# A named ScalarE table for logarithm and exponential in gated linear attention, and one pair of evictions moved

## The reference, cut to what matters

```python
la_f = jax.nn.log_sigmoid(lr_f @ w_g_f + b_g_f) / GLA_TAU      # gate, both directions
b = jnp.cumsum(gc, axis=-2)                                    # per chunk of 64 tokens
q_in = qc * jnp.exp(b - ref);  k_in = kc * jnp.exp(ref - b)
q_inter = qc * jnp.exp(b);     k_state = kc * jnp.exp(b_last - b)
decay = jnp.exp(b_last[..., 0, :])
...
o = rmsnorm(o_f + o_b, out_norm)                               # y / sqrt(mean(y*y) + eps)
y_gla = gla_branch(...) * jax.nn.silu(gate_g)
y_mla = mla_branch(...) * jax.nn.silu(gate_a)
```

## Time and profile before

| what | value |
|---|---|
| median of 3 runs | 2426.88 us (2423.91 to 2427.3) |
| profiled execution, its own time | 2427.41 us |
| its span, first to last instruction | 2425.6 us |
| PE busy | 2254.9 us, 93% of the span |
| DVE busy | 1390.4 us, 57% |
| ACT busy | 1132.1 us, 47% |
| POOL busy | 488.1 us, 20% |
| mean granted TensorE clock | 0.975 |

### The profile page before, as it was taken

One profiled execution on the slowest core, in us unless ns is written; L12 is line 12 of the kernel. 1 busy time (PEld: TensorE's weight loads), 2 busy tenths in 40 slices (PEclk: granted clock), 3 DMA queues, 4 the chain that ended last, 5 costly groups with the idle time before them and its releaser, 6 DMA issues.

```text
span 2425.6 us, 30125 instructions
## 1 busy us (share of the span) xinstructions
PE 2254.9 (93%) x11196; PEld 1781.9 (73%) x11196; DVE 1390.4 (57%) x2137; ACT 1132.1 (47%) x1768; POOL 488.1 (20%) x512
## 2 busy tenths in 40 slices
PE   8998888988999993999999999999899999999998
PEld 4777555864777762777877888888777877888886
DVE  4578378325777766367426776354457526776353
ACT  5222377223666654566453445245656453445142
POOL 1046434111223222311230002001211230002000
PEclk9999999999999995999999999999999999999999
DMA  6200120124999976111110003112111110003112
GB/s 204 100 35 1 57 83 1 11 104 163 381 395 381 340 295 227 40 31 35 36 46 22 12 28 133 49 53 100 41 36 35 35 46 22 12 10 133 67 52 96
DMA packets 148397, 239.56 MB, mean 99 GB/s; under 512 B 45232, under 2 KB 101808, under 8 KB 136368
## 3 DMA queue, kind: packets, MB, share of 16 engines
q1 hardware_dynamic: 138304, 221.07, 25.9%
q0 software_dynamic: 8928, 16.80, 1.8%
q10 hardware_dynamic: 1040, 0.00, 0.0%
HBM read 212.13 MB, written 41.42 MB: 105 GB/s over the span
## 4 chain that ended last, share of the span: by engine, by line
PE 52%; ACT 4%; DVE 3%; issue 2%; POOL 1%; DMA 0%; POOLq 0%; ACTq 0%; DVEq 0%
PE ps L105 11%; PE ps L106 11%; PE ps L107 11%; PE ps L95 4%; PE ps L1998 2%; PE ps L1952 1%; PE ps L1951 1%; PE ps L1950 1%; PE ps L1989 1%; PE ps L1988 1%; PE ps L1986 1%; PE ps L1985 1%; PE ps L1987 1%; PE ps L524 1%; PE ps L1866 1%
## 5 line engine op out<-in xcount | busy, mean ns | idle before, releaser
L107 PE MATMUL ps<-HT_hi,WF_lo 128*128 128x512 f32 x800 | 314.6, 393 | 0.0
L105 PE MATMUL ps<-HT_hi,WU_hi 128*128 128x512 f32 x704 | 285.3, 405 | 18.7 <-POOL WF_lo L1028 6.4
L106 PE MATMUL ps<-H_lo,WU_hi 128*128 128x512 f32 x704 | 276.5, 393 | 0.0
L106 PE MATMUL ps<-WT_lo,HT_hi 128*128 128x512 f32 x664 | 260.5, 392 | 0.0
L1028 POOL TENSOR_TENSOR WF_lo<-WF,WU_hi 128x1024 fp32r<-128x1024 f32 x42 | 110.8, 2638 | 466.2 <-ACT WU_hi L1299 466.2
L105 PE MATMUL ps<-W_hi,HT_hi 128*128 128x512 f32 x472 | 186.9, 396 | 2.9 <-DVE WT_lo L2568 2.9
L107 PE MATMUL ps<-W_hi,MIX_lo 128*128 128x512 f32 x480 | 188.4, 393 | 0.0
L107 PEld LDWEIGHTS ps<-HT_hi,WF_lo 128*128 128x128 f32 x800 | 151.8, 190 | 32.6
L105 PEld LDWEIGHTS ps<-HT_hi,WU_hi 128*128 128x128 f32 x704 | 133.9, 190 | 52.6 <-POOL WF_lo L1028 8.6
L106 PEld LDWEIGHTS ps<-H_lo,WU_hi 128*128 128x128 f32 x704 | 134.0, 190 | 29.5 <-issue 2.9
L106 PEld LDWEIGHTS ps<-WT_lo,HT_hi 128*128 128x128 f32 x664 | 125.8, 190 | 25.6 <-issue 0.5
(11 more groups left out here) (482 smaller groups left out, 5682.7 us busy)
## 6 DMA issues: line engine op xcount, KB each, us to landing
WT<-in_w_gate SPq DMA_DIRECT2D x31, 1024.0 KB
WT<-in_w_up SPq DMA_DIRECT2D x31, 1024.0 KB
MIX<-in_w_down SPq DMA_DIRECT2D x31, 1024.0 KB
WF<-in_w_in SPq DMA_DIRECT2D x48, 512.0 KB, 3.9
WT<-in_w_out SPq DMA_DIRECT2D x6, 2048.0 KB, 8.5
H<-in_x SPq DMA_DIRECT2D x16, 512.0 KB, 9.3
h_dram<-H SPq DMA_DIRECT2D x16, 512.0 KB, 2.8
H<-h_dram SPq DMA_DIRECT2D x16, 512.0 KB, 11.8
```

Of the source, the lines that this page charges most:

```text
L105: pe.matmul(o, lh, rh, start=(i == 0), stop=False)
L106: pe.matmul(o, lh, rl, start=False, stop=False)
L107: mm = pe.matmul(o, ll, rh, start=False, stop=(i == last))
```

## The change

ACT is told by name to load a table that holds both logarithm and exponential: once at the start of each layer, after each `gg` unit and after `ga1`. The builder then finds both functions in the table in place, and loads another only for SiLU (and later for the softmax and the sigmoid). In `gg2`, whose `between` is `rms(1)`, the weights' high part and `rms(1)` now come ahead of the first half's SiLU, directly behind the wait for that half, so that SiLU isn't called on both sides of the logarithm.

```diff
+LOG_EXP = "natural_log_exp_and_others"
...
                 rows_hi(act, L, NT - 1)
                 unit_hi(L, 1)
+                act.preload_act_table_set(LOG_EXP)
                 act.wait_ge(vl_ready, L + 1)
...
                         act.wait_ge(u_ready, L * 2 * NU + 2 * u + half + 1)
+                        if (kind, i, half) == ("gg", 2, 0):
+                            unit_hi(L, u + 1)
+                            between()
...
-                        if 1 <= u < NU - 1 and half == 0:
-                            unit_hi(L, u + 1)
-                        if half == 0 and between is not None:
-                            between()
+                        if half == 0 and (kind, i) != ("gg", 2):
+                            if 1 <= u < NU - 1:
+                                unit_hi(L, u + 1)
+                            if between is not None:
+                                between()
+                    if kind == "gg" or (kind, i) == ("ga", 1):
+                        act.preload_act_table_set(LOG_EXP)
```

## The result

| | median us | range, executions | ratio to before, 95% interval |
|---|---|---|---|
| before | 2427.09 | 2423.91 to 2428.14, 4 | |
| changed | 2406.44 | 2405.23 to 2409.08, 4 | 0.9919 (0.9901 to 0.9936) |
| before, another chip | 2428.81 | 2424.41 to 2437.35, 11 | |
| changed, that chip | 2407.91 | 2405.16 to 2409.88, 6 | 0.9915 (0.9899 to 0.993) |

What follows compares the result with a forecast made beforehand. PE, busy 93% of the span, was taken as the bound, so ACT savings count only at PE's waits. Waits of 8.24 us plus 1.47 for the clock gave 9.71 us per layer, 19.4 in both: 2407.5 us, range 2403.5 to 2414.5.

Steps and rivals of the forecast that it cites:

- The loads: ACT's table loads in the stage: 18 fewer per layer, 36 x 1.283 = 46.2 us of ACT in all.
- Rival 4: The builder keeps its loads and the named ones come on top; gaps stay, 2427 us; chance 0.05.
- A: At `gate(0)`: PE's wait for the low part of the weights of `gg0` goes, 2.26 us per layer.
- rival 2: Another wait replaces the removed one (POOL loses the port or DVE is late for `inner(0)`): 2412.0 us; chance 0.10.
- B: At `gate(1)` and `gate(3)`: PE's wait for the value tile's eviction shrinks by 1.69 us each, 3.38 us per layer.
- C: At `rms(0)`: the wait of `inner(1)` for the inverse root goes, 1.42 us per layer.
- D: At `finish(0)` and `finish(2)`: the 0.59 us waits of the transposes of `la` go, 1.18 us per layer.
- E: The granted clock's short fall behind the `gate(3)` gap goes, 1.47 us per layer; bounds 0 and 1.47 us.
- Rival 1: The clock falls elsewhere instead: 2410.4 us, or 2413.4 us with a further fall in each layer; chance 0.25.
- Rival 3: Two more clock falls vanish, each 1.47 us, and small seams close: 2404.5 us; chance 0.08.
- The moved step: At `gg2`: first half evicted by 1125.0, wanted when the transposes end at 1129.2; margin 4 us, nothing lost.
- Rival 5: Named table slow to load: gain gone at t = 6.3 us per load, 2437.6 us at t = 9 us; chance 0.02.

Runs made afterwards that it cites:

- move-only kernel: Changed kernel with all named table loads taken out and the new order at `gg2` kept; 2427.07 us, ratio to before 0.9997.
- table only: Changed kernel with the named loads kept and the evictions of `gg2` in the old order; 2409.91 us, ratio to before 0.9928.
- four hidden: Changed kernel with four more table loads behind `gg0` and four behind `gg2`, ahead of the copy of the keys; 2405.31 us, one execution.
- no SiLU: Changed kernel with SiLU of `gg` and `ga` replaced by a plain copy and the loads behind them left out; 2409.71 us, one execution.
- weights first: Changed kernel with the weights' high part copied ahead of the first half's eviction at `gq0` and `gk0`; 2406.34 us, ratio to before 0.9906.
- two experiments: The table only run and the move-only kernel, by which the new order at `gg2` is worth about 0.1 us per layer.

## Why the prediction was right, point by point

**The loads.** 36 fewer were forecast and 36 are gone; the 46.2 us of ACT are 45.1 in its busy time. Rival 4 (the loads stay) is out.

**A.** Forecast 2.26 us, measured 2.34 when its loads are put back. The collision of POOL and DVE moved along whole, so rival 2 is out: no wait took the removed one's place. The forecast put POOL's end 2.57 us ahead of its old one; from the start of `gates(0)` it is 1013.03 - 999.95 = 13.08 us after and 1017.15 - 1001.53 = 15.62 before, so 2.54 us. That new start times can make POOL and DVE hold each other up came true at `gate(1)` and `gate(3)` (last section), where PE had no wait for it.

**B.** Forecast 1.69 us for each gap. PE's wait shrank from 1.94 to 0.25, and comes back as 1.93 with the loads at `gate(3)`. The forecast 2 us in all for the eight waits is measured 2.0. Put back one at a time, the gaps make the ruler 1.6 us longer each.

**C and D.** Both waits went; with the loads back at `rms(0)` they return at 1.4 and 0.6 us. Only `finish(0)` was tried by itself; `finish(2)` is read from the group's being gone.

**E.** Forecast 1.47 us per layer, kept. With loads put back, a fall again cost 1.5 or 1.6 us, but the gap doesn't fix its coming. Before, both layers had the gaps of `gate(0)` and `gate(1)` without a fall and that of `gate(3)` with one; put back alone, `gate(0)` and `gate(3)` brought it in L = 1 only and `gate(1)` in both. The move-only kernel, with all gaps in place, repeats the kernel before in both layers. Of these eighteen gaps of 1.9 to 2.3 us eight brought a fall. The reverse holds without exception: the six traces without such a gap (the changed kernel on both chips, table only, four hidden, no SiLU, weights first) have no fall in any of their twelve rulers. What was right was to price it as gained where the gap goes. The Trainium skill (TensorE: Matmul & The Clock Gate, "Part 1") says that the chip looks at activity on a grid that doesn't follow the kernel; the equal gaps of 1.93 us with and without a fall agree. It doesn't explain why with all gaps in place the fall came behind `gate(3)` four times out of four; what decides it no run here shows. Rival 1 (the fall comes elsewhere) didn't happen in the stage: no fall is in either ruler. Rival 3 is not needed: the sum accounts for the ruler.

**The sum.** 9.71 us per layer, measured 10.1 and 10.2. The 0.4 us over are seams. Where a wait stood, the next matmul now starts before the one ahead of it ends (1013.27 against 1012.69 + 0.66 = 1013.35), which my sum of waits left out: 0.08 us at A and 0.07 each at C and twice at D. Another 0.2 us, of which 0.1 are lost again behind them, lie at head 2's transposes, where the prediction saw no gap to close. First two rows before, then two after:

```profile
1125.96 2.06 PE L1850 MATMUL ps<-X,WT 64*128 64x128 f32 x32
1128.15 1.06 PE L1856 MATMUL ps<-ident,X 128*128 128x128 f32 x8
...
1118.26 2.06 PE L1858 MATMUL ps<-X,WT 64*128 64x128 f32 x32
1120.24 1.09 PE L1864 MATMUL ps<-ident,X 128*128 128x128 f32 x8
```

From the scores to the transposes it was 2.19 us, 0.13 of them idle, and it is 1.98.

**The moved step.** Forecast as nothing lost, and so it is; it gains the 0.1 us of the two experiments. Its margin was forecast as 4 us and is 4.2 by the rows; no experiment went up to it.

**Rival 5's price.** Here a step of mine was wrong, though nothing hung on it. I took the idle time of ACT ahead of `ks_copy` as the room for a load. That is the time in which ACT waits for PE, but what counts is when PE wants the copy: with four more loads (5.1 us) against the 1.11 us of idle time that the changed kernel has left in both places, the rule's price is 4.0 us each at `gg0` and at `gg2`, and the measured is 0. So the point t = 6.3 us, at which the gain was to be gone, doesn't stand as it was worked out: that much ACT time at these two places is free. What so long a load would cost at the other four named places of a layer, which the sum left out, no run shows.

## What to carry to other kernels

Put two functions that alternate on ScalarE under one table by name, and count the gain only where TensorE waits: 46.2 us of loads here gave 20 us of time, each term but the clock's read from one wait. The room for an added ScalarE step reaches to the first instruction that wants what is queued behind it, not to the end of ScalarE's own idle time. A TensorE gap that goes may take a fall of the clock with it, and the same gap brought it in one layer and not in the other, so it is a separate term with a chance of its own.

## What the runs showed of the hardware that was not expected

A table load is 1.283 us in every group of these traces, whichever table it brings, and the next instruction on ACT, where it waits for nothing else, follows 0.01 to 0.02 us later. Four in a row took 5.17 us. The Trainium skill (ScalarE: Activation LUTs, "What ACT_TABLE_LOAD costs") gives about 1283 ns for the load, which agrees, and about 1380 ns more for a drain with each switch. The trace doesn't show the drain; by it four loads would take about 10.6 us (an estimate from that page), so the measurement decides.

Behind `gate(3)`, in the changed kernel, POOL's subtraction of the weights and a small DVE copy of 64 x 16, which otherwise takes 0.17 us, now lie over each other, in both layers:

```profile
1145.89 2.18 DVE L2454 COPY marks<-X 64x16 f32<-64x16 f32 x1
```

It ends about when POOL's operation does, at 1148.04 (start 1143.67, 4.37 us). This is more of the collision of the earlier trace rows. POOL's operation was 3.12 us at this place before. At `gate(1)` such a pair lay over each other before as well (the copy took 2.19 us, POOL's operation 2.77); there the copy stayed at 2.17 us and POOL's went to 4.45. These four operations, two in each layer, are in the main what raises POOL's mean from 2.638 to 2.750 us; PE didn't wait for them and lost nothing.
